# Turning the gated attention output by DMA instead of by TensorE

## The reference, cut to what matters

```python
def one_chunk(args):                      # 64 queries see their own chunk and 8 before
    s = einsum('bqhd,bkhd->bhqk', qb, kb) * scale + bias
    s = where(valid, s, MASK_VALUE)
    p = softmax(s, axis=-1)
    return einsum('bhqk,bkhd->bqhd', p, vb)
...
y_attn = chunked_rel_attention(qh, kh, vh, rel_bias) * silu(attn_g)
y = concatenate([y_pool, y_attn], axis=-1)
x = x + einsum('bse,ed->bsd', y, w_out)
return rms_norm(x, final_norm_gain)
```

## Time and profile before

| | |
|---|---|
| median of 3 runs | 1643.2 us (1640.18 to 1643.58) |
| profiled execution | 1641.95 us |
| its span, first to last instruction | 1640.2 us |
| mean granted TensorE clock | 0.993 |
| PE busy | 1575.8 us (96%) |
| DVE, ScalarE (ACT), GpSimd (POOL) busy | 1036.2, 826.0, 665.0 us |
| DMA packets on the queue that SP feeds | 61.1% of 16 engines' span |

### The profile page before, as it was taken

How to read it: one execution, slowest core, us unless ns; L and a number is a source line. 1 busy time by engine, 2 the same in 40 slices (tenths; PEclk the granted TensorE clock), 3 DMA queues, 4 the chain that set the end, 5 groups by cost and what they waited for, 6 DMA issues and landing times.

```text
span 1640.2 us, 42712 instructions
## 1 busy us (share of the span) xinstructions
PE 1575.8 (96%) x17344; PEld 1178.5 (72%) x17344; DVE 1036.2 (63%) x2134; ACT 826.0 (50%) x1541; POOL 665.0 (41%) x666
## 2 busy tenths in 40 slices
PE   7999999999999999999987899999999999999976
PEld 3455455468677777767766788998888898888854
DVE  7977867747565566556435566666666666666665
ACT  6655555522121111112125677676776776776774
POOL 2543433311101111111313466556665666655654
PEclk9999999999999999999999999999999999999989
DMA  6556556473514533542764788777778767778664
GB/s 248 214 193 219 195 207 219 179 269 136 218 66 172 201 112 134 180 169 89 219 213 118 173 201 204 183 190 172 190 200 199 196 177 176 191 194 201 162 166 107
DMA packets 296987, 297.37 MB, mean 181 GB/s; under 512 B 169912, under 2 KB 230344, under 8 KB 294744
## 3 DMA queue, kind: packets, MB, share of 16 engines
q1 hardware_dynamic: 296264, 293.99, 61.1%
q0 software_dynamic: 528, 0.66, 0.3%
HBM read 150.87 MB, written 83.54 MB: 143 GB/s over the span
## 4 chain that ended last, share of the span: by engine, by line
PE 60%; SPq 6%; DMA 5%; POOL 4%; ACT 3%; issue 2%; DVE 1%; DVEq 0%; ACTq 0%; POOLq 0%
PE bank L1154 9%; PE bank L1996 6%; PE bank L1130 6%; PE bank L1133 6%; PE bank L1132 6%; DMA stages<-rows 5%; PE bank L1739 4%; PE bank L1742 4%; PE bank L1741 4%; PE bank L1919 3%; SPq L2419 2%; POOL stages L2354 2%; PE bank L2050 2%; PE bank L2052 2%; PE bank L2051 2%
## 5 line engine op out<-in xcount | busy, mean ns | idle before, releaser
L1739 PE MATMUL bank<-middle,weights 128*128 128x128 f16 x1792 | 310.0, 219 | 8.8 <-ACT middle L1749 4.1
L1741 PE MATMUL bank<-middle,weights 128*128 128x128 f16 x1792 | 309.7, 219 | 0.0
L1742 PE MATMUL bank<-middle,weights 128*128 128x128 f16 x1792 | 309.7, 219 | 0.0
L2370 POOL TENSOR_TENSOR rows<-rows 128x640 f16<-128x640 f32 (+4 forms) x128 | 174.1, 1360 | 281.5 <-ACT rows L2173 281.5
L1130 PE MATMUL bank<-middle 128*128 128x256 f16 x784 | 213.7, 273 | 0.5 <-DVE stages L1270 0.5
L1132 PE MATMUL bank<-middle 128*128 128x256 f16 x784 | 213.7, 273 | 0.0
L1133 PE MATMUL bank<-middle 128*128 128x256 f16 x784 | 213.7, 273 | 0.0
L1996 PE MATMUL bank<-entry,stages 128*128 128x512 f16 x768 | 186.0, 379 | 0.7 <-DVE stages L2237 0.7
L1739 PEld LDWEIGHTS bank<-middle,weights 128*128 128x128 f16 x1792 | 175.4, 98 | 11.3 <-issue 4.4
L1741 PEld LDWEIGHTS bank<-middle,weights 128*128 128x128 f16 x1792 | 175.5, 98 | 0.4
L1742 PEld LDWEIGHTS bank<-middle,weights 128*128 128x128 f16 x1792 | 175.4, 98 | 0.0
(11 more groups left out here) (168 smaller groups left out, 3952.3 us busy)
## 6 DMA issues: line engine op xcount, KB each, us to landing
entry<-in_x SPq DMA_DIRECT2D x64, 512.0 KB, 3.7
h_ops<-middle SPq DMA_DIRECT2D x16, 1792.0 KB, 6.1
middle<-h_ops SPq DMA_DIRECT2D x112, 256.0 KB, 5.5
middle<-h_ops SPq DMA_DIRECT2D x49, 512.0 KB, 7.5
residual<-entry SPq DMA_DIRECT2D x32, 512.0 KB, 2.7
middle<-middle SPq DMA_DIRECT2D x128, 128.0 KB, 3.1
out<-entry SPq DMA_DIRECT2D x31, 512.0 KB, 3.1
entry<-residual SPq DMA_DIRECT2D x30, 512.0 KB, 5.4
```

The source lines that it names most:

```text
L1739: nc.tensor.matmul(dst, wh, hop3[:, o, 0, kt, :], start=(kt == 0 and s < 2 and pair == 0), stop=False, skip_group_check=True)
L1741: nc.tensor.matmul(dst, wh, hop3[:, o, 1, kt, :], start=False, stop=False, skip_group_check=True)
L1742: mm = nc.tensor.matmul(dst, wl, hop3[:, o, 0, kt, :], start=False, stop=(kt == 3), skip_group_check=True)
L2370: nc.gpsimd.tensor_tensor(r16[:, j, 1, c:640], r32[:, j, c:640], r16[:, j, 0, c:640], ALU.subtract).then_inc(A["rpl_done"], 1)
```

## The change

For the tiles 0 to 14 the two rounds on PE go. ScalarE writes the high halves of y (without a scale) into a new tile y16 (`turn_hi`), GpSimd the low halves (`turn_lo`), and SP turns y16 by one DMA transpose of 8 blocks (`turn_y`) into yT; there are two such turns a tile, for heads 0 to 3 at the end of head 5, and for heads 4 to 7 at the end of head 0 of the next tile. `output` waits for both. The scale of y moves into the column of ones (2 / YS). The last tile keeps its rounds on PE. For the tiles 0 and 1 a row head's turn is now one transpose of 20 blocks as well (r16 is zeroed first), the first of them is issued at the end of the q phase, and ScalarE's and GpSimd's row work of j = 0 comes last in its head. The buffer for dynamic DMA descriptors is halved, and y16 takes its place.

```diff
-SCRATCH = 4096
+SCRATCH = 2048
+        y16 = sb("branch_halves", [P, 2, 2, 2 * P], F16)
-                             1.0).then_inc(H["consts"], 1)
+                             2 / YS).then_inc(H["consts"], 1)
...
+            turn(sp, 0, 1)
             for s in range(2):
                 sp.wait_ge(r_stored[s], 16 * 2 * PTILES)
...
         def round_at(t, h):
-            if t > 0 and h < 2:
-                return t - 1, h
             return {HALF + 1: (t, 0), HEADS - 1: (t, 1)}.get(h) if t == LAST else None
+        def turn_at(t, h):
+            if h == 0 and t > 0:
+                return t - 1, 1
+            return (t, 0) if h == HALF + 1 and t < LAST else None
...
+            nc.gpsimd.memset(r16[:, :, :, :], 0.0).then_inc(A["mask_rows"], 1)
...
                 if first == 0:
-                    pe.wait_ge(A["ytl_done"], 2 * t + (1 if t == LAST else 2))
+                    if t == LAST:
+                        pe.wait_ge(A["ytl_done"], 1)
+                    else:
+                        pe.wait_ge(y_turned, 32 * (t + 1))
...
+            def turn_hi(t, r):
+                act.wait_ge(A["ya_done"], 2 * (HEADS * t + HALF * (r + 1)))
+                at_least(act, y_turned, 16 * (2 * t + r))
+                nc.scalar.activation(y16[:, 0, ...], y[...], ACT.Copy).then_inc(A["yth16_done"], 1)
...
         # ScalarE, end of head(t, h)
                 if round_at(t, h):
                     branch_hi(*round_at(t, h))
+                if turn_at(t, h):
+                    turn_hi(*turn_at(t, h))
                 other(t, h, 2)
...
+                if by_rows(h) and t < 2:
+                    row_exponential(t2, h2, 0)
...
+            def turn_lo(t, r):
+                pool.wait_ge(A["yth16_done"], 2 * t + r + 1)
+                nc.gpsimd.tensor_tensor(y16[:, 1, ...], y[...], y16[:, 0, ...],
+                                        ALU.subtract).then_inc(A["ytl16_done"], 1)
...
         # GpSimd, end of head(t, h)
                     if split_at(t, h):
                         kq_lo(pool, split_at(t, h))
+                    if turn_at(t, h):
+                        turn_lo(*turn_at(t, h))
...
+            def turn_y(t, r):
+                sp.wait_ge(A["ytl16_done"], 2 * t + r + 1)
+                at_least(sp, A["out_mm"], 4 * t)
+                sp.dma_start_transpose(yT[:, r, ...], y16[...]).then_inc(y_turned, 16)
...
                     for j in range(2):
                         load_residual(t - 1, j)
+                    turn_y(t - 1, 1)
...
                 if t > 0:
                     store(t - 1, 0)
+                turn_y(t, 0)
-                turn(t, 7)
+                turn(sp, t, 7)
```

More of the change, by code:

```diff
@@ L1563, in build @@
             shift_done rexp_done rph_done rpl_done max_mm max_done mrow_mm mrow_done st_mm bias_done exp_done ph_done pl_done
-            pv_mm rc_done ya_done yt_mm yth_done ytl_done ss_done ms_done rstd_done fin_done""".split()
+            pv_mm rc_done ya_done yt_mm yth_done ytl_done yth16_done ytl16_done ss_done ms_done rstd_done fin_done""".split()
         A = {n: sem("a_" + n) for n in names}
-        wob_loaded = [sem(f"a_wob_loaded{n}") for n in range(NKT)]
+        wob_loaded = [sem(f"a_wob_loaded{n}") for n in range(2)]
         hop3_loaded = entry_loaded
         turned = sem("a_turned")
+        y_turned = sem("a_y_turned")
         moved_k = [sem(f"a_moved_k{s}") for s in range(2)]
@@ L1674, in round_at, with turned_part @@
         def round_at(t, h):
-            if t > 0 and h < 2:
-                return t - 1, h
             return {HALF + 1: (t, 0), HEADS - 1: (t, 1)}.get(h) if t == LAST else None
+        def turn_at(t, h):
+            if h == 0 and t > 0:
+                return t - 1, 1
+            return (t, 0) if h == HALF + 1 and t < LAST else None
+        def turned_part(part, kts):
+            first = kts.start
+            return yT[:, first // 2, part, first % 2:first % 2 + kts.stop - first, :]
         def round_kts(t, r):
@@ L1870, in move_k, with turn @@
                     sp.dma_start(ks[DH:P, r, o, h2, :], nat[rows, 0, 0, h2, :]).then_inc(moved_k[half], 16)
+        def turn(sp, t, h):
+            head = HEADS * t + h
+            if head == 1:
+                sp.wait_ge(A["mask_rows"], 2 * (RING // 2) + 3)
+            sp.wait_ge(A["rpl_done"], row_count(t, h, 1) + 1)
+            at_least(sp, A["pv_mm"], head - 1)
+            sp.dma_start_transpose(pT[:, :, :, :, :].rearrange("p j a i n -> p (j a i) n"),
+                                   r16[:, :, :, :].rearrange("p j a n -> p (j a n)")).then_inc(turned, 16)
         def before(t, h, g):
@@ L1932, in max_rows @@
                 if back >= 0 and round_at(t, back):
-                    of, r = round_at(t, back)
-                    pe.wait_ge(A["ytl_done"], 2 * of + r + 1)
+                    _, r = round_at(t, back)
+                    pe.wait_ge(A["ytl_done"], r + 1)
             for j in range(2):
@@ L2204, in head @@
                         max_row(t1, h1)
-                    if t2 < ATILES:
+                    if t2 < ATILES and t >= 2:
                         row_exponential(t2, h2, 0)
@@ L2234, in branch_lo @@
             def branch_lo(t, r):
-                dve.wait_ge(A["yth_done"], 2 * t + r + 1)
+                dve.wait_ge(A["yth_done"], r + 1)
                 first, end = round_kts(t, r)
[L2237 to L2240, removed]
+                nc.vector.tensor_tensor(
+                    turned_part(1, slice(first, end)),
+                    tra[:, 0:(end - first) * AT].rearrange("p (k n) -> p k n", k=end - first),
+                    turned_part(0, slice(first, end)), ALU.subtract).then_inc(A["ytl_done"], 1)
             def add_bias(t, h):
@@ L2375, in a_phase_pool @@
                 for h in range(HEADS):
+                    t2, h2 = ahead(t, h, 2)
                     if by_rows(h):
-                        t2, h2 = ahead(t, h, 2)
                         for of, j in finish_at(t, h):
                             rstd(of, j)
-                        if t2 < ATILES:
+                        if t2 < ATILES and t >= 2:
                             row_lo(t2, h2, 0)
@@ L2394, in a_phase_pool @@
                         kq_lo(pool, split_at(t, h))
+                    if turn_at(t, h):
+                        turn_lo(*turn_at(t, h))
+                    if by_rows(h) and t < 2:
+                        row_lo(t2, h2, 0)
             for j in range(2):
@@ L2406, in store @@
                 sp.dma_start(out_blk[2 * t + j], res[:, j, :]).then_inc(out_stored[j], 16)
[L2408 to L2419, removed]
+            def turn_y(t, r):
+                sp.wait_ge(A["ytl16_done"], 2 * t + r + 1)
+                at_least(sp, A["out_mm"], 4 * t)
+                sp.dma_start_transpose(yT[:, r, :, :, :].rearrange("p a k (j n) -> p (a k j) n", j=2),
+                                       y16[:, :, :, :].rearrange("p a k n -> p (a k n)")).then_inc(y_turned, 16)
             def load_wob(n):
                 at_least(sp, A["wob_lo"], n - 1)
-                sp.dma_start(res[:, n % 2, :], wout_v[NKT + n]).then_inc(wob_loaded[n], 16)
+                sp.dma_start(res[:, n % 2, :], wout_v[NKT + n]).then_inc(wob_loaded[n % 2], 16)
             for t in range(ATILES):
@@ L2430, in a_phase_sp @@
                         load_hop3(sp, 2, s)
-                    turn(t, 1)
                     load_wob(2)
@@ L2438, in a_phase_sp @@
                 else:
-                    turn(t, 1)
+                    turn(sp, t, 1)
                     load_v(sp, t, 1)
@@ L2457, in a_phase_sp @@
                         if s == 2:
-                            turn(t, 3)
+                            turn(sp, t, 3)
                 else:
-                    turn(t, 3)
+                    turn(sp, t, 3)
                 move_k(sp, t + 1, 0)
                 move_q(sp, t + 1, 0)
-                turn(t, 5)
+                turn(sp, t, 5)
                 load_v(sp, t + 1, 0)
```

38 lines of the change are left out of this document (22 added, 16 removed).

## The result

The changed kernel takes 1690.02 us (median of 4, 1688.43 to 1691.25) against 1641.97 us (median of 4, 1640.18 to 1643.58): ratio 1.0293, 95% interval 1.0277 to 1.0308. Its profiled execution took 1688.43 us with a span of 1686.6 us, 46.4 us longer than the span before.

What follows compares the result with a forecast made beforehand. PE was taken to bound the middle tiles. 13 projections x (2.6 + 1.0) = +46.8, with -10 + 3 + 2 for the ends, made +41.8 us, so 1684 us; range 1648 to 1702, 1663 to 1703 for this case alone.

Steps and rivals of the forecast that it cites:

- the ends: Tiles 0 and 1 and the last tile: -10 us, +3 for tile 1's projection wait, +2 for the last tile.
- PE bounds the middle, one for one: Tiles 2 to 13: PE waits only 2.7 us, so PE's time counts fully; dropping its transposes saves 0.88 us a tile.
- The new wait: Before each tile's projection in head 2, PE waits 3.5 us for y's second turn; each tile 2.6 us longer.
- The clock: Behind the new waits PE runs at half clock for a time: 1.0 us a tile, between 0 and 1.7.
- The rival in which the clock holds: Middle tiles: the new waits bring no half clock, +29 us, 1671 us; chance 0.20.
- ScalarE and GpSimd: Writing y's halves at the ends of heads 0 and 5: counted 0, at most 0.5 us a tile.
- the cover: End of head 5: ScalarE's 0.59 us and GpSimd's 1.43 us of idle time were to hide the new halves.
- A middle tile in all: Tiles 1 to 13: 2.6 us from the wait plus 1.0 us from the clock for each projection.
- Tiles 0 and 1: Single larger turns shorten the chain in which ScalarE waited 27.7 us: -10 us, between -3 and -16.
- The +3 for that wait: Tile 1: its projection of tile 0 now waits for y too, +3 us, between 0 and +6.
- The last tile: Its projection of tile 14 waits too, where PE idles anyway: +2 us, between -1 and +5.
- No wait for y: Middle tiles: the residual loads do not hold up y's turn, so the kernel gets faster, -20 us, 1622 us; chance 0.14.

Runs made afterwards that it cites:

- e1: Changed kernel with SP issuing the second turn of y before the two residual loads instead of behind them: 1637.52 us, ratio 0.9965 to the kernel before.
- e2: Changed kernel with the second turn of y issued between the two residual loads: 1659.62 us, ratio 1.0084 to the kernel before.
- e9: e6 with the last four operand loads of a tile issued behind the turn of head 5: 1627.56 us, ratio 0.9901 to the kernel before.
- e3: Changed kernel with 40 filler matmuls on PE just before it waits for the turn of y: 1682.91 us, ratio 1.0231 to the kernel before.
- e5: e1 with head 5's high and low halves of y moved ahead of the row work: 1634.01 us, ratio 0.9942 to the kernel before.
- e6: e5 with the second turn of y issued ahead of the gate load too: 1632.60 us, ratio 0.9932 to the kernel before.
- e4: Kernel before with only the change's part for tiles 0 and 1 and the halved descriptor buffer, y still turned by PE: 1634.57 us, ratio 0.9938.
- e10: e4 with the same four operand loads moved behind the turn of head 5, y turned by PE: 1633.23 us, ratio 0.9938 to the kernel before.
- e8: Changed kernel with only head 5's halves moved ahead of the row work, turn of y still behind the residual loads: 1685.42 us, ratio 1.0255.

## Why the prediction was right

The forecast was 1684 us for a cause, a place and a size, and 1690 came out. The cause and the place are shown by e1 and e2. That the number came so near is in part luck: the middle tiles were counted 5.2 us too dear and the ends 9.7 us too cheap. Point by point:

- **PE bounds the middle, one for one.** Held. The period of a tile without any wait went from 48.87 to 47.97 us (e9), 0.90, where 0.88 were counted for the transposes. (The 48.8 us of the prediction are such periods; the mean was 49.14.)
- **The new wait.** Held in mechanism: y lands behind the residual loads. Its size was 3.5 us a tile and measured 3.0 (38.8 in 13). In tile 7 the operand load landed 0.7 us behind the second residual load (1203.17), and 0.5 were added for a transpose, 1.2 in all; the turn came 1.0 us behind it in the mean. The rest of the difference has no run of its own.
- **The clock.** Counted 1.0 us a tile, measured 0.8 (e3) to 0.9 (the rows). Of the 14 waits of tiles 0 to 13 six had a stretch of half clock behind them or around them, although nearly all were between 2.4 and 3.7 us. The rival in which the clock holds did not come.
- **ScalarE and GpSimd.** Counted 0, with 0.5 us a tile as the bound. In the changed kernel 3.8 us in 4 tiles. Freed of the wait for y it shows as 7.0 (e1). The step that failed is the cover: of ScalarE's 0.6 us at the end of head 5 "nearly all" was to be covered, and the marks of e1 and e5 show that 0.5 us were not. They cost PE only in tiles whose turn of head 5 lands late, 2.7 us in all in e1. What the sum had no term for is that SP's loads come closer to the projection and make that turn later (the other 1.8 us that e1 has over the kernel before). It is not the 1.25 us of issuing that `turn_y` takes: behind it SP sat idle 1.3 to 3.3 us in front of head 3's turn in e1, e5 and e6. In the changed kernel the price was small, since PE stood still anyway. GpSimd's low half took 1.2 us, the lower end of what was counted.
- **A middle tile in all.** 3.6 us counted, 3.2 measured: from the projection of tile 1 to that of tile 13 it was 589.72 us and is 628.18, +38.5 in twelve periods.
- **Tiles 0 and 1.** -10 counted, -9 to -10 measured by e4. At the projection of tile 1 e4 was 6.8 us earlier than before, and the changed kernel should have been too, but for its wait. The +3 for that wait was too small: it was 4.9 us, with half clock around it. The projection of tile 1 starts 1.2 us later than before (957.28 to 958.51); less that tile's own 3.2, this end gave -2.0 where -7 was counted.
- **The last tile.** +2 counted, +6.7 measured: the wait there was 5.8 us, above what I had read for the landing. That PE idles later in that tile did not take it up. This stretch is the least certain of them: in the profiled executions of the other kernels it runs from 92.8 (e10) to 100.6 us (e5), and e4, without a wait for y, has 97.6. The sum is 13 x 3.2 - 2.0 + 6.7 = +46.3, where I had +41.8: the ends were 9.7 us too low and the middle 5.2 too high.
- **No wait for y** was the rival with the other sign, 1622 us. In e6 and e9 PE's waits for y in the middle tiles are gone (1632.6 and 1627.6), and what that needed was another place in the queue. The 1622 was not reached: the waits for GpSimd take part of it.

## What to carry to other kernels

A transfer that replaces a step on an engine can get more of its time from the queue in which it stands than from its own size: here the same turn landed after 3.1 us with nothing large ahead and after 6.8 behind two loads. Look up, in the trace of before, when the transfer that now stands in that place lands, and compare it with the first instruction that will wait. Count what the loads around it do to the next urgent transfer as well, and look which issue behind it had no idle time in front. If the freed engine was the bound, as here, a wait on it costs its length and, behind some waits, the slower clock; if such a wait is there anyway, other late work hides behind it and comes out when it is gone.

## What the runs showed that I had not expected

- An engine that only issues can be the bound of a step: in e6 SP's issues followed one another from the turn of head 3 to that of head 5, and a transpose's issue stretched to 4.7 us behind the loads, against 3.0 at the shortest.
- At the shortest, a turn of 8 blocks costs SP 1.25 us and a turn of 20 blocks 3.0; the four small ones of tiles 0 and 1 together took 5.0 to 6.3. Here one larger transpose was cheaper than four small ones, although a part of what it turns is zeros (e4, -9 us, together with the moved first turn and row work). In a quiet queue 8 blocks landed 3.1 us after the issue and 20 blocks 4.9: 393 KB more in 1.8 us, 218 GB/s by this estimate, next to the 215 of the earlier trace rows.
- A wait of 2.4 to 3.7 us brought TensorE's clock to half behind some and not behind others, and the changed kernel's period was 50.7 us in one tile and 54.7 in another. In e8, with waits as long, nine of the 13 had a stretch of half clock beside them. What tells the cases apart is open.
